# A YOCO decoder step whose attention stage is rebuilt: queries and values split earlier, negated scores, narrower causal blocks, norms on GpSimd

## The reference, cut to what matters

```
x = LN(a*x + conv_mixer(x)); x = LN(a*x + ffn0(x))         # layer 0
k, v = split(x @ kv_w); logf = log_sigmoid(x @ f_w + f_b); C = cumsum(logf)
q = x @ w_q
s[t, u] = q_t.k_u / 8 + C[t] - C[u]   for u <= t, else -inf # per head
o = softmax(s) @ v
x = LN(a*x + o @ w_o); x = LN(a*x + ffn1(x))                # layer 1
```

## Time and profile before

| what | value |
|---|---|
| median of 3 runs | 2944.03 us (2940.56 to 2947.19) |
| span of the profiled execution | 2939.8 us |
| mean granted TensorE clock | 0.951 |
| busy: PE, PEld, DVE, ACT, POOL | 93%, 89%, 44%, 29%, 28% |
| projection stage kvq (from its first unit to its last) | about 1256 to 1544.9 us |
| between its last unit and the first score | 1544.9 to 1574.1 us |
| attention | 1574.1 to 1979.8 us |

### The profile page before, as it was taken

One profiled execution on the slowest core, in us unless ns is written; L12 is line 12 of the kernel. 1 busy time (PEld: TensorE's weight loads), 2 busy tenths in 40 slices (PEclk: granted clock), 3 DMA queues, 4 the chain that ended last, 5 costly groups with the idle time before them and its releaser, 6 DMA issues.

```text
span 2939.8 us, 44825 instructions
## 1 busy us (share of the span) xinstructions
PE 2726.8 (93%) x16971; PEld 2622.2 (89%) x16971; DVE 1279.7 (44%) x2212; ACT 838.0 (29%) x1463; POOL 822.3 (28%) x475
## 2 busy tenths in 40 slices
PE   8999959999999999699996889989799999999994
PEld 8999949999999999499994777779699999999994
DVE  3333582422222222850555888874733222222237
ACT  2111142111111111432224666652511111111114
POOL 2222252112212112532333333323612221212114
PEclk9999979999999999899997888889799999999996
DMA  4111101111111111022874454442011111111101
GB/s 131 43 50 43 45 22 44 44 44 44 46 56 44 51 44 44 15 74 77 262 245 129 125 133 124 123 126 65 22 44 44 44 57 45 51 44 44 51 15 58
DMA packets 214332, 206.47 MB, mean 70 GB/s; under 512 B 29239, under 2 KB 184887, under 8 KB 214188
## 3 DMA queue, kind: packets, MB, share of 16 engines
q1 hardware_dynamic: 209388, 187.25, 21.8%
q0 software_dynamic: 4800, 17.08, 1.7%
HBM read 178.76 MB, written 25.57 MB: 70 GB/s over the span
## 4 chain that ended last, share of the span: by engine, by line
PE 80%; DVE 10%; issue 5%; DMA 2%; ACT 1%; POOL 1%; SPq 0%; DVEq 0%; POOLq 0%; ACTq 0%
PE ps L1600 25%; PE ps L1601 24%; PE ps L1602 24%; DVE ss L1482 2%; PE ps L1859 2%; DVE ln_t L1271 1%; DVE ln_t L1275 1%; PE ps L1888 1%; DVE ln_d L1216 1%; DVE ptl L1507 1%; DMA k_prompt<-ktok 1%; PE ps L1874 1%; PE ps L1841 1%; PE ps L1837 1%; PE ps L1875 1%
## 5 line engine op out<-in xcount | busy, mean ns | idle before, releaser
L1600 PE MATMUL ps<-xh,whi 128*128 128x344 f32 x3288 | 1067.7, 325 | 28.2 <-POOL xl L663 18.0
L1601 PE MATMUL ps<-xl,whi 128*128 128x344 f32 x3288 | 1054.7, 321 | 0.0
L1602 PE MATMUL ps<-xh,wlo 128*128 128x344 f32 x3288 | 1054.5, 321 | 0.0
L617 POOL TENSOR_TENSOR wlo<-wraw,whi 128x1024 fp32r<-128x1024 f32 x197 | 481.3, 2448 | 1700.4 <-ACT whi L794 1700.4
L1600 PEld LDWEIGHTS ps<-xh,whi 128*128 128x128 f32 x3288 | 620.2, 189 | 56.8 <-POOL xl L663 34.3
L1602 PEld LDWEIGHTS ps<-xh,wlo 128*128 128x128 f32 x3288 | 621.8, 189 | 0.0
L1601 PEld LDWEIGHTS ps<-xl,whi 128*128 128x128 f32 x3288 | 621.6, 189 | 0.0
L1600 PE MATMUL ps<-zh,whi 128*128 128x344 f32 x1440 | 465.4, 323 | 17.4 <-DVE x L1343 9.4
L1601 PE MATMUL ps<-zl,whi 128*128 128x344 f32 x1440 | 463.7, 322 | 0.0
L1602 PE MATMUL ps<-zh,wlo 128*128 128x344 f32 x1440 | 461.7, 321 | 0.0
L1320 DVE TENSOR_TENSOR silu<-silu,ps 128x344 f32<-128x344 f32 x132 | 67.8, 513 | 875.6 <-PE ps L1602 875.6
(11 more groups left out here) (206 smaller groups left out, 2650.0 us busy)
## 6 DMA issues: line engine op xcount, KB each, us to landing
wraw<-ffn_w_gu SPq DMA_DIRECT2D x88, 512.0 KB, 3.8
wraw<-ffn_w_down SPq DMA_DIRECT2D x44, 512.0 KB, 3.5
kp<-cache_k SPq DMA_DIRECT2D x32, 512.0 KB, 5.4
vp<-cache_v SPq DMA_DIRECT2D x32, 512.0 KB, 3.5
wraw<-a_w_in SPq DMA_DIRECT2D x24, 512.0 KB, 3.8
wraw<-kv_w SPq DMA_DIRECT2D x16, 512.0 KB, 5.3
qd<-q_t SPq DMA_DIRECT2D x32, 256.0 KB, 4.7
kd<-k_t SPq DMA_DIRECT2D x32, 256.0 KB, 5.3
```

The lines of the kernel that those rows point to most:

```text
L617: pool.tensor_tensor(wlo[:, s, :], wraw[:, s, :], f32(whi[:, s, :]), ALU.subtract).then_inc(w_lo, 1)
L1600: pe.matmul(out, w_h, m_h, start=start, stop=False)
L1601: pe.matmul(out, w_h, m_l, start=False, stop=False)
L1602: return pe.matmul(out, w_l, m_h, start=False, stop=stop)
```

## The change

1. **Ring.** `wraw` now lies on the same memory as `wlo`, and `low` subtracts in place. So `load` of slot n waits for the unit that used slot n - 3 to end on TensorE (`used`, or `ffn_released` in the FFN), no longer for its `whi` and `wlo` to be made. The slot of `f_w` is split in its 16 columns alone.
2. **kvq.** In queries ACT takes q negated and rounded to `hl` (one buffer), VectorE makes the low part from PSUM (`q_low`) and it is VectorE's instruction that frees the chunk. POOL stores high and low (1 MB per block, before 0.5 MB). ACT takes a block only when the store before has landed. v is also written split (`vst`), by ACT and VectorE, and stored as `v_t` (1 MB per block) beside `v_prompt`. VectorE's `q_low` and `v_low` of the queries come behind the residual loop in its order.
3. **Attention.** q and v are loaded split. Scores are negated, so the drain takes a minimum which is the exponent's bias as it stands (`exps` with scale -1) and `nm`'s instruction is gone. For t = 0 the last 128 keys are not computed, drained, exponentiated or transposed, and the last v block multiplies 128 queries. All norms are `tensor_scalar` on POOL. k high is made on POOL too (`k_split`: a copy and a subtraction).
4. **Output.** ACT copies all 128 partitions of the output (`o_take`). SP stores one half, and POOL adds the other half to it in DRAM by an accumulating DMA (`add_halves`). The last pair is added as before. `oraw` has 5 slots instead of 8; blocks 5 and 6 are loaded when slots 0 and 1 have been split, and block 7 is taken from `ost` in SBUF.

```
-        W_AT = ZL_AT + WIDE
-        M_AT = W_AT + 3 * WR * WCOLS * 4
+        W_AT = Z_END + 3 * KB * 512
+        M_AT = W_AT + 2 * WR * WCOLS * 4
+        wraw = Area(W_AT + WR * WCOLS * 4).put("wraw", [P, WR, WCOLS], F32)
...
-                    sp.wait_ge(w_hi, taken)
-                    sp.wait_ge(w_lo, taken)
+                    sp.wait_ge(done, count)
+            def used(unit):
+                return full[NCH - 1], unit - WR + 1
...
+            def take_q(it, j):
+                if j or not (isinstance(it, int) and it == 0):
+                    act.wait_ge(kv["qdma"], 16 * x)
+                for c in range(NCH):
+                    act.wait_ge(full[c], g + 1)
+                    act.activation(hl[:, 0, ...], ps[:, c, 0:w], ACT.Copy, scale=-QSCALE).then_inc(kv["qh"], 1)
...
+            def q_low(it, j):
+                for c in range(NCH):
+                    dve.wait_ge(kv["qh"], NCH * x + c + 1)
+                    dve.scalar_tensor_tensor(hl[:, 1, ...], ps[:, c, 0:w], -QSCALE, f32(hl[:, 0, ...]),
+                                             ALU.mult, ALU.subtract).then_inc(free[c], 1)
+            with dve.Fori(0, KB // 2) as it:
+                q_low(it, 0)
+                v_low(it)
+                q_low(it, 1)
...
             with dve.Fori(0, NS // 2) as it:
+                v_low(it + KB // 2)
...
+            def k_split(b, e):
+                pool.wait_ge(qk_in[e], loaded)
+                pool.tensor_copy(kh[e][:, :], kd[e][:, :]).then_inc(at["khi"], 1)
+                pool.wait_ge(at["khi"], 2 * b + e + 1)
                 pool.tensor_tensor(kl[e][:, :], kd[e][:, :], f32(kh[e][:, :]), ALU.subtract).then_inc(at["klo"], 1)
+            def norm(b, st):
+                pool.wait_ge(at["rinv"], inverted)
+                for t in range(2):
+                    pool.tensor_scalar(ss[j][:, t, 0:span(st, t)], ..., ri[:, j, t:t + 1], None,
+                                       ALU.mult).then_inc(at["pnorm"], 1)
+            def add_halves(b, e):
+                pool.wait_ge(oe_st[e], 16 * (b + 1))
+                pool.dma_start(o_t[...], oe[e][DH:P, :], accum_op=ALU.add).then_inc(oe_add[e], 16)
+            with pool.Fori(0, KB - 1) as b:
+                norm(b, STEPS)
+                k_split(b + 1, 0)
+                for st in range(STEPS + 1, PAIR):
+                    norm(b, st)
+                add_halves(b, 0)
+                norm(b, PAIR)
+                k_split(b + 1, 1)
+                for st in range(PAIR + 1, PAIR + STEPS):
+                    norm(b, st)
+                add_halves(b, 1)
...
+            with sp.Fori(0, KB - 1) as b:
+                next_qk(b, 0)
+                load_v_page(b, 2)
+                load_v_page(b, 3)
+                next_qk(b, 1)
+                next_v(b, 0)
                 store_head(b, 0)
+                load_v_page(b + 1, 0)
+                load_v_page(b + 1, 1)
+                next_v(b, 1)
                 store_head(b, 1)
...
-                dve.tensor_tensor_reduce(ss[j][:, t, :], ...[:, 0:2 * P * width(st)],
-                                         ncb[...], 1.0, -3e38, ALU.add, ALU.max, mx[:, j, t:t + 1])
-                if t == 1:
-                    dve.tensor_scalar(nm[:, j, :], mx[:, j, :], -1.0, None, ALU.mult)
+                dve.tensor_tensor_reduce(ss[j][:, t, 0:span(st, t)], ...[:, 0:span(st, t)],
+                                         ncb[...], 1.0, 3e38, ALU.add, ALU.min, nm[:, j, t:t + 1])
...
+def span(st, t):
+    return P * (2 * (st % STEPS) + t + 1)
+def turned(st, g):
+    return P * (3 if g == st % STEPS else 4)
```

More of the change, by code:

```diff
@@ L231, in build @@
         ftok = fa.put("ftok", [P, TB + 1, H], F32)
+        assert fa.at <= SC_AT
         aa = Area(XH_AT)
[L234 to L239, removed]
@@ L244, in build @@
[L244 to L250, removed]
+        pth = [area.put(f"pth{i}", [P, TB * 2 * P], F32R) for i, area in enumerate((za, aa))]
+        ptl = [area.put(f"ptl{i}", [P, TB * 2 * P], F32R) for i, area in enumerate((za, aa))]
+        assert aa.at <= ZH_AT and za.at <= PAGES_AT - 3 * D * 4
+        oa = Area(ZL_AT + 6 * ROW)
@@ L355, in ffn_released @@
                 grp, r = grp - 1, r + 6
+            if isinstance(grp, int) and grp == 0 and r == 3:
+                return full[NCH - 1], UNITS[st] + 2
             if r in (2, 3):
@@ L437, in _ @@
+                group(1)
+                with sp.Fori(2, FG) as grp:
+                    group(grp)
+                n = n0 + 4 + 6 * (FG - 1)
+                down(n, n0 + 4, FG - 1, 0, ffn_released(l, FG, 0 - WR))
+                down(n, n0 + 4, FG - 1, 1, ffn_released(l, FG, 1 - WR))
             load_ffn(0)
-            load(SLOTS["f"], SLOTS["f"], w_f, cols=H)
-            n0 = SLOTS["kvq"]
+            load(SLOTS["f"], SLOTS["f"], w_f, ffn_released(0, FG - 1, 5), cols=H)
+            n0, g0 = SLOTS["kvq"], UNITS["kvq"]
@@ L678, in _ @@
             ffn_low(0)
-            n0 = SLOTS["kvq"]
-            low(n0 - 1, n0 - 1)
+            n0, g0 = SLOTS["kvq"], UNITS["kvq"]
+            low(n0 - 1, n0 - 1, cols=H)
             ln_sums(1)
@@ L749, in head @@
-            def head(b, e, last=False):
-                for j in range(2):
-                    for t in range(2):
-                        norm(b, e, j, t)
-                if not last:
-                    k_low(b + e, 1 - e)
-                norm(b, e, 2, 0)
-                if not last:
-                    v_low(b + e, 1 - e)
-            k_low(0, 0)
-            v_low(0, 0)
-            with pool.Fori(0, KB - 1) as b:
-                head(b, 0)
-                head(b, 1)
-            head(KB - 1, 0)
@@ new lines, in add_halves @@
+            def add_halves(b, e):
+                pool.wait_ge(oe_st[e], 16 * (b + 1))
+                pool.dma_start(o_t[bass.ds(b, 1), e * DH:(e + 1) * DH, :].rearrange("a p t -> (a p) t"),
+                               oe[e][DH:P, :], accum_op=ALU.add).then_inc(oe_add[e], 16)
+            k_split(0, 0)
+            norm(0, 0)
+            k_split(0, 1)
+            for st in range(1, STEPS):
+                norm(0, st)
+            with pool.Fori(0, KB - 1) as b:
+                norm(b, STEPS)
[8 more added lines that the diff above has]
+                add_halves(b, 1)
@@ L768, in _ @@
+            for st in range(STEPS, PAIR):
+                norm(KB - 1, st)
             proj_low("o", 2)
@@ L1520, in step @@
             def step(b, st, last=False):
-                if st % PAIR == 0:
-                    q_low(b + st // PAIR, 1)
-                if st == STEPS and not last:
-                    q_low(b + 1, 0)
                 for g in range(STEPS):
@@ L1533, in step @@
                     inverse(b, st + 2)
-                    norm(b, st + 2)
-                if st >= 2:
-                    o_sum(b, st - 2)
+                if last and st >= 2:
+                    o_sum(st - 2)
             def sample_sum(b):
```

538 lines of the change are left out of this document (298 added, 240 removed).

## The result

The changed kernel takes **2964.45 us** (median of 4 runs, 2961.01 to 2968.03) against 2944.66 of the kernel before in the same comparison: ratio **1.0067**, 95% interval 1.0053 to 1.0081. It is slower by 20 us where I forecast 20 faster. The profiled execution has a span of 2959.3 (before 2939.8), 19.5 more.

A forecast was written before the change was run, and what follows sets the result against it. The prediction took attention to be bound by TensorE and VectorE waiting on each other. Attention -72, first query +24.5, keys +16 and end of kvq +11.5 made -20 us: 2944.0 to 2924, range 2876 to 2966.

The forecast's parts named there:

- What bounds the kernel, and VectorE's relief: Attention: TensorE waits on VectorE's ptl; VectorE falls from 42 to some 25 us per pair, no bound any more.
- The pair, TensorE's side: Attention: TensorE's floor 34 us, plus 3 idle and 3.5 low clock, makes a pair 40.5, before 49.5; gain 72.
- the narrow widths: Attention, TensorE's floor per head: 0.4 us less for transposes, 0.6 for masked keys and half a mask, 0.15 for values.
- GpSimd in a pair: Attention: norms 17.6 us, k splits 7.3 to 9.7, DMAs 2; 27 to 29 of 40.5, so not the bound.
- The rule on GpSimd: Attention: the skill page speaks against the move; its line rate would about halve the norms' 17.6 us; sum unmoved.
- First query: kvq, first query: q_low waits behind VectorE's residual loop, ending near 1302; TensorE stalls 22 us, 24.5 with clock and late take.
- Keys: kvq, keys: waits for slot 2's load and SP's pages cost 5.3 us at each of three transitions: 16, bounds 6 and 27.
- End of kvq: End of kvq: the last eight pages come after TensorE's last unit; +11.5 us to the first score, 9 to 16.
- Ring: Weight slots in projections, FFNs and layer norms: later loads stay hidden or even out; net 0, -4 to +6 us.
- The slower rival: Attention, GpSimd's queue: loads landing in 10 us make turns wait 5 us per pair; p = 45.5, 2964 us; 20%.
- p: Attention: the new pair's time in us; 40.5 forecast, break-even at 43.
- The signs: For wrong: turns waiting for GpSimd's norm, FFN units waiting for low, pair above 43, or attention's clock still 0.87.

The follow-up runs named there:

- e2: The changed kernel with each of GpSimd's norms working on 2 columns only, instructions and waits kept; ratio 0.9964 to the kernel before.
- e10: As e1, with both accumulating DMAs also issued one norm later; ratio 0.9958 to the kernel before.
- e1: The changed kernel with GpSimd's norms as tensor_tensor with the factor broadcast, in place of tensor_scalar; ratio 0.9982 to the kernel before.
- e3: The changed kernel with the norms of the j = 3 steps moved to VectorE, behind the reciprocal; ratio 1.0063 to the kernel before.
- e5: The changed kernel with VectorE's residual loop behind the lows of the first queries iteration; ratio 1.0005 to the kernel before.
- e6: The changed kernel with SP's page loads placed between the weight loads in keys; ratio 1.0043 to the kernel before.
- e9: The changed kernel with ScalarE's ktok copies ahead of high of slot 2 in keys, GpSimd's order likewise; ratio 1.0091 to the kernel before.
- e11: The changed kernel with the changes of e10, e5, e6 and e9 together; 2893.1 us, ratio 0.9819 to the kernel before.

## Why the prediction was wrong

- **What bounds the kernel, and VectorE's relief: right.** In attention VectorE is busy 196.9 us, 135 less than in the earlier trace rows, where I had some 140 less (124, and 2 per pair for the narrower work). The matmuls' wait for `ptl` fell to 4.6 us; the weight loads' wait for it stayed.
- **The pair, TensorE's side: right as a sum, by luck in parts.** Without the norms' load it is 40 (e2), and with the short form and the waits moved attention is 336.0 (e10), against 405.7 - 72 = 333.7 forecast. So of the 34 us that attention missed, e1 and e10 give back 32. Within it the narrow widths give 0.7 per pair and not 2.3, and the clock comes back further than I had it in the middle of e2, to 1.00, and to 0.98 from 1700 to 1940 in e10.
- **GpSimd in a pair: the step that failed.** I wrote "27 to 29 of 40.5, so it is not the bound". The row behind it was of a tensor_tensor with the factor broadcast; the change uses tensor_scalar, and I priced it as the same. It measures 2202 ns against 1469 for 768 columns, 28.7 us per pair against my 17.6. Scaling one row by its columns was short even for the old form, which measures 19.4 (the narrow ones have a fixed part: 671 ns for 128 columns). With 28.7 in its place my own sum would have been 38 to 40.4 of 40.5. And it booked none of the queue's blocking waits: 6.0 per pair, for the loads ahead of `k_split` and for the store ahead of the accumulating DMA. Without the overlaps GpSimd's work and these waits take 41.8 per pair, over my 40.5, so the pair could not reach it. e1 shows the form's share, 25 us, e10 attention 6 us less by the waits. The k splits (7.2, bounds 7.3 to 9.7) and DMA issues (1.7, priced 2) were close.
- **The rule on GpSimd.** The Trainium skill, "GPSIMD Engine Reference", section 4.1, calls one-input work roughly line rate and two-input work about twice slower. For 1024 columns the trace has 1178 ns for the cast, with one input, and 2404 for the subtraction, with two, which fits. It does not fit the norm: 2843 ns as tensor_scalar, with one tensor input, and 1895 as tensor_tensor with the factor broadcast. So the form has to be priced, not only its inputs. The section's advice, to keep elementwise work on VectorE, is borne out by the price (747 ns there for the same norm), though moving the long norms back gained nothing by itself (e3).
- **First query: 17.6 idle, I wrote 22.** The log-forget chain did slip, as I had it for slot 2's load: its last instruction starts at 1282.98, before at 1278.41. But the residual loop behind it took 15.1 us, where it had taken 19.4, and ended at 1298.2, not 1302. I had taken its old length over. In the kernel before, two of its sixteen instructions took 3.31 and 3.48 us, the other six of their kind 1.23, and both ran beside a `low` of GpSimd:

```profile
1281.21 3.31 DVE L1404 SCALAR_TENSOR_TENSOR x<-xl,x 128x1032 f32<-128x1032 f32 x1
...
1292.67 3.48 DVE L1404 SCALAR_TENSOR_TENSOR x<-xl,x 128x1032 f32<-128x1032 f32 x1
```

```profile
1280.47 2.96 POOL L617 TENSOR_TENSOR wlo<-wraw,whi 128x1024 fp32r<-128x1024 f32 x1 [8.07 <-ACT whi L794]
...
1292.65 2.39 POOL L617 TENSOR_TENSOR wlo<-wraw,whi 128x1024 fp32r<-128x1024 f32 x1 [7.41 <-ACT whi L794]
```

In the changed kernel no `low` runs from 1276.5 to 1302.7, and all eight take 1.23. That the loop holds the chunk is shown by e5.

- **Keys: 5.64, 4.80 and 4.87, I wrote 5.3 each.** I had named both causes, the load of slot 2 and SP's pages, and said that the second ends near where the first has put it. e6, e9 and e11 bear that out, with the second one unit later. I left out the low clock behind these stalls; with it kvq came to 42.3 against my 40.5 in spite of the shorter first stall, so the close total is partly luck.
- **End of kvq: +15.3, I wrote +11.5**, near the upper bound of 16. The last score ended 30.8 us after the last unit, where I took 29, and the first score of attention came 13.9 behind it, where I had 11.3 to 11.5. The DMA share was 0.93 there, so the queues were not empty, as I had assumed; no run shows that this is the cause.
- **Ring: 0 outside kvq, right:** all other stretches together differ by 0.4 us.
- **The slower rival** gave 2964 and p = 45.5 by this very queue, but by another step of it: a load 2.5 us later than I had it. In e2 the waits for loads and stores grow (34.6 and 78.3 us in 300) and hold nothing up, so waits alone don't make the bound. With the norm's own row this rival was the one to take. That it gave the measured time is partly luck: 8 x (49.5 - 44.0) = 44 against kvq's 57.6 would be +14, and 20 was measured. Attention gained 38 and not 44, and 3 of these 6 lie in the first pair: from the first score to its fourth sample page it took 60.0 us before and 57.8 after.
- **The signs.** Two of those that I had written for being wrong came: turns that wait for GpSimd's norm, and a pair period above 43.

## What to carry to other kernels

An instruction that moves to another engine needs a price for its own form on that engine; a row of another form with the same shapes was off by half. Add up an engine's queue with its blocking waits, since in an in-order queue a wait for a DMA costs what stands behind it: shorter work there can turn into a longer wait with no gain at all (e3). And when two waits lie beside each other, each fix alone can measure as nothing (e6 and e9, neither clear of the noise), while with both in place the stalls went, so try the pair before dropping either.

## What the runs showed of the hardware

- GpSimd's multiplication by a per-partition factor: as tensor_scalar 886, 1562 and 2843 ns for 128, 512 and 1024 columns, some 2.5 ns per column more from 512 to 1024; as tensor_tensor with the factor broadcast 671, 1041 and 1895, some 1.7. A cast of 1024 columns took 1178, a subtraction 2404.
- VectorE's fp32 instruction with two tensor inputs over 1032 columns took 1.23 us, and 3.3 to 3.5 in the two cases that ran beside a subtraction of GpSimd.
- A stall of TensorE costs more than its length: after 17.6 us of idle time the granted clock was 0.76 over the next 11.3 us. In kvq 32.9 us of stalls came with 10.1 us more busy time of TensorE for the same units.
- Issuing an accumulating DMA took GpSimd 0.87 us, and its wait for the first half's landing stood on the chain that ended last (8.9% of it from 1690 to 1955).
